# Another idle pattern and another order of the first products in a two-layer encoder trunk

## What is computed

```
def hybrid_layer(x, ...):
    u = rms_norm(x, g_mix_pre)
    proj = u @ w_in            # split into qa, ka, va, cq, ckv, ga, gb
    ...                        # two attentions, gated sum
    x = x + rms_norm(mixed @ w_out, g_mix_post)
    h = rms_norm(x, g_mlp_pre)
    h = jnp.square(jax.nn.relu(h @ w_mlp_in)) @ w_mlp_out
    return x + rms_norm(h, g_mlp_post)
```

## Time and profile before

| | us |
|---|---|
| median of 3 runs | 745.71 |
| lowest and highest run | 745.63, 745.94 |
| the profiled execution | 745.94 |
| its span, first to last instruction | 744.1 |

### The profile page before, as it was taken

The page is one execution under the profiler, slowest core; times in us unless marked ns, Lnnn a source line. Parts: engine busy times, 40 slices in busy tenths (PEclk is TensorE's granted clock), DMA queues, the critical chain, the costliest instruction groups (busy, mean ns, idle before and its releaser), DMA issues.

```text
span 744.1 us, 10940 instructions
## 1 busy us (share of the span) xinstructions
PE 733.6 (99%) x3986; PEld 622.5 (84%) x3986; DVE 503.7 (68%) x710; ACT 415.1 (56%) x783; POOL 157.6 (21%) x256
## 2 busy tenths in 40 slices
PE   8999999999999999999999999999999999999996
PEld 7988888888788888888888888888887888888885
DVE  5787777666775656656686776876668665665664
ACT  6867765343654544444576786644447454455452
POOL 1991432000130111110137513310003110011110
PEclk9999999999999999999999999999999999999999
DMA  7767534455456555456348755346364646655611
GB/s 263 203 211 246 198 114 145 168 198 170 147 193 203 193 177 201 150 204 212 106 115 245 244 162 206 114 135 206 113 226 145 214 153 223 214 181 186 204 62 57
DMA packets 79500, 132.18 MB, mean 178 GB/s; under 512 B 15290, under 2 KB 21476, under 8 KB 79204
## 3 DMA queue, kind: packets, MB, share of 16 engines
q1 hardware_dynamic: 79188, 131.64, 54.0%
q10 hardware_dynamic: 272, 0.00, 0.0%
HBM read 130.59 MB, written 1.05 MB: 177 GB/s over the span
## 4 chain that ended last, share of the span: by engine, by line
PE 94%; DVE 4%; ACT 1%; issue 0%; POOL 0%; DMA 0%; POOLq 0%; ACTq 0%; DVEq 0%
PE acc L1420 17%; PE acc L1422 17%; PE acc L1421 17%; PE sc L1767 7%; PE tp L1767 6%; PE tp L1395 4%; PE sc L1770 3%; PE acc L1454 3%; PE tp L1770 3%; PE sc L1420 3%; PE sc L1422 2%; PE sc L1421 2%; DVE w_lo L1046 2%; PE sc L1552 1%; PE sc L1540 1%; DVE x L1223 1%
## 5 line engine op out<-in xcount | busy, mean ns | idle before, releaser
L1046 DVE TENSOR_TENSOR w_lo<-raw,w_hi 128x1024 fp32r<-128x1024 f32 (+4 forms) x256 | 305.4, 1213 | 152.2 <-ACT w_hi L707 151.3
L707 ACT CAST w_hi<-raw 128x1024 fp32r<-128x1024 f32 (+4 forms) x256 | 250.7, 999 | 173.9 <-PE acc L1422 95.4
L1420 PE MATMUL acc<-w_hi,s_hi 128*128 128x512 f32 x288 | 112.2, 390 | 0.0
L1421 PE MATMUL acc<-w_lo,s_hi 128*128 128x512 f32 x288 | 112.1, 389 | 0.0
L1422 PE MATMUL acc<-w_hi,s_lo 128*128 128x512 f32 x288 | 112.0, 389 | 0.0
L1420 PE MATMUL acc<-w_hi,s_both 128*128 128x512 f32 (+2 forms) x288 | 108.3, 376 | 0.0
L1422 PE MATMUL acc<-w_hi,s_both 128*128 128x512 f32 (+2 forms) x288 | 105.9, 368 | 0.0
L1421 PE MATMUL acc<-w_lo,s_both 128*128 128x512 f32 (+2 forms) x288 | 105.8, 367 | 0.0
L567 POOL TENSOR_TENSOR tok<-relu_h 128x512 f32<-128x512 f32 x32 | 37.0, 1160 | 262.8 <-ACT relu_h L808 257.8
L1767 PE MATMUL sc<-s_both,w_hi 128*128 128x512 f32 x224 | 70.4, 395 | 0.0
L1422 PEld LDWEIGHTS acc<-w_hi,s_lo 128*128 128x128 f32 x288 | 54.1, 188 | 11.3
(11 more groups left out here) (210 smaller groups left out, 1149.8 us busy)
## 6 DMA issues: line engine op xcount, KB each, us to landing
raw<-in_w_mlp_in SPq DMA_DIRECT2D x32, 1024.0 KB, 5.4
raw<-in_w_mlp_out SPq DMA_DIRECT2D x32, 1024.0 KB, 5.0
raw<-in_w_in SPq DMA_DIRECT2D x24, 1024.0 KB, 5.3
raw<-in_w_oa SPq DMA_DIRECT2D x8, 1024.0 KB, 5.0
raw<-in_w_out SPq DMA_DIRECT2D x8, 1024.0 KB, 5.0
raw<-in_w_ob SPq DMA_DIRECT2D x4, 1024.0 KB, 4.9
raw<-in_w_in SPq DMA_DIRECT2D x3, 768.0 KB, 4.6
raw<-in_w_in SPq DMA_DIRECT2D x4, 576.0 KB, 6.2
```

Of the source, the lines that this page charges most:

```text
L707: s.copy(high, src).then_inc(hi_ready, 1)
L1046: v.tensor_tensor(low, src, high, ALU.subtract).then_inc(lo_ready, 1)
L1420: mm(banks[t][:, 0:N], h[:, kk, tk], wh[:, k, :], start=(start and k == 0), stop=False)
L1421: mm(banks[t][:, 0:N], h[:, kk, tk], wl[:, k, :], start=False, stop=False)
```

## The change

Three things change, all in layer 0's head.

The first weight piece is cast by VectorE instead of ScalarE, after the angles; ScalarE starts at piece 1 and first waits for VectorE's cast, so that `hi_ready` counts in order.

In `first_product`, piece 1's high x high products and piece 0's low-weight products now stand ahead of the turn of x's second half; only piece 1's low-weight products stay behind it. This order of the products holds for every call; the turn is there in layer 0's first call alone.

The six plain idle products behind the turn of x's first half become fifteen in the split format fp32r: three with 128 moving columns, six with 64 and six with 256. Their operand is a copy of the identity in that format, twice side by side, made by GpSimd.

```
+        ident_r = sb("ident_r", [P, 2, P], F32R)
...
+            g.tensor_copy(ident_r[:, :, :], ident[:, :].unsqueeze(1).to_broadcast([P, 2, P])).then_inc(ident_r_ready, 1)
...
-                    if pos.l == 0 and pos.j is None and p == 0:
-                        act.wait_ge(first_loaded, 16)
-                    elif p % 2 == 0 or p == 1:
+                    if pos.l == 0 and pos.j is None and p == 1:
+
+                        act.wait_ge(hi_ready, 1)
+                    if p % 2 == 0 or p == 1:
...
                     turned_hi(pos, ("x", 0, 0))
+                    state[0] = 1
                     hi(pos, 1)
...
                     take_angles()
+                    dve.wait_ge(first_loaded, 16)
+                    dve.wait_ge(piece_used, 1)
+                    v.tensor_copy(split_view(w_hi, 0), raw_view(0)).then_inc(hi_ready, 1)
                     lo(pos, 1)
...
+            def idle_split_products():
+
+                pe.wait_ge(ident_r_ready, 1)
+                for _ in range(3):
+                    mm(acc[3][:, 0:P], ident_r[:, 0, :], ident_r[:, 0, :], start=True, stop=True)
+                for _ in range(6):
+                    mm(acc[3][:, 0:CHUNK], ident_r[:, 0, :], ident_r[:, 0, 0:CHUNK], start=True, stop=True)
+                for _ in range(6):
+                    mm(acc[3][:, 0:SEQ], ident_r[:, 0, :], ident_r[:, :, :], start=True, stop=True)
...
                     turn_x(pos, kind, 0, (0,))
-                    idle_product(6)
-                part(0, s1_hi, w_hi, [0], first=True)
+                    idle_split_products()
+                part(0, s1_hi, w_hi, range(2), first=True)
+                part(0, s1_hi, w_lo, [0])
                 if not turned0:
                     turn_x(pos, kind, 0, (1,))
-                part(0, s1_hi, w_hi, [1])
-                part(0, s1_hi, w_lo, range(2))
+                part(0, s1_hi, w_lo, [1])
```

More of the change, by code:

```diff
@@ L295, in build @@
         ident_ready = sem("ident_ready")
+        ident_r_ready = sem("ident_r_ready")
         consts_ready = sem("consts_ready")
```

## The result

| | us |
|---|---|
| before, median of 8 runs | 745.64 (745.45 to 745.94) |
| after, median of 8 runs | 748.2 (746.26 to 748.5) |
| ratio | 1.0029, 95% interval 1.0020 to 1.0039 |
| profiled execution of after, its span | 747.63, 745.8 |

The change costs 2.6 us by the medians, 0.34%; the ratio of 1.0029 lies nearer to that of the means. The forecast was +1.0. One more number in the table matters: before, the runs lie within 0.5 us; after, seven lie at 747.6 to 748.5 and one at 746.26. The profiled execution is 1.7 us longer in its span than that of before (744.1).

A forecast was written before the change was run, and what follows sets the result against it. TensorE bounds the kernel and passes the head's delay on whole. Idle products 0.64 plus products ahead of the turn 1.16 minus 0.78 gave +1.02 us: 746.96 on the profiled execution, 746.7 on the median; range 745.8 to 748.4.

The forecast's parts named there:

- main case: Layer 0's head: idle loads at 0.213 us, real products at 0.175, turn 1.02 us later; +0.8 to +1.4, chance 0.5.
- What bounds the kernel, and that the head passes its delay on: Whole span: TensorE, busy for 99%, bounds it; any delay it has at 20 us reaches the end whole.
- The critical event, the turn of x's second half: Head: ScalarE idles 0.86 us before 9.56 waiting for this turn, then copies out and casts pieces 2 and 3.
- Fifteen idle loads at 0.213: Idle products on TensorE: 15 x 0.213 = 3.20 us, ending at 8.79 instead of 8.15, 0.64 us later.
- The order: `first_product`: a load and six products ahead of the turn take 1.16 us where two took 0.78.
- The clock stays as before: TensorE's head: clock low up to some 8.8 us, high after, so the six products run at 0.175 us each.
- The missed rise: Rival: clock stays low past the turn, which starts 2.0 and ends 2.5 us late; +2.5, 748.2; chance 0.25.
- The cheap rival, narrow products at 0.107: Idle products: loads don't slow with the clock, or columns alone count; +0.44 (746.15) or +0.35; chance 0.2.
- The cast: VectorE casts piece 0 in 0.6 us (lower bound 0.56), ending at 6.5; ScalarE's added wait is already met.
- The cover: Head: piece 0's cast ends at 6.5, 6.9 at the longest, while TensorE's idle products run to 8.79.
- GpSimd's copy: Identity's split copy takes 0.8 us, ending about 3.5; TensorE asks for it at 5.6: hidden, no cost.
- No gain has a path in the head: Head: the order allows the turn at most 0.1 us earlier; no gain above 0.2%, chance of one 0.04.

The follow-up runs named there:

- cast_only: Kernel before with only VectorE casting piece 0 and ScalarE starting at piece 1; idle products and order kept: 745.59 us, ratio 1.0001.
- before_wide12: Kernel before with its twelve plain idle instructions replaced by twelve split idle products of 256 columns: 745.39 us, ratio 0.9997.
- after_narrow15: Changed kernel with all fifteen split idle products 64 columns wide: 748.12 us, ratio 1.0031.
- idle_only: Kernel before with only the fifteen split idle products in place of the twelve plain idle instructions; casts and order kept: 746.69 us, ratio 1.0007.
- after_plain15: Changed kernel with seven plain idle products (fourteen weight loads) and one split one of 256 columns: 746.04 us, ratio 1.0008.

## Why the prediction was right in its range and wrong in its main case

**What bounds the kernel, and that the head passes its delay on**: right. The delay at piece 3, 1.77 us, is the growth of the span, 1.7, and from the restart of TensorE with piece 3 to the end of the span all twelve traces of this case take 731.6 to 731.9 us.

**The critical event, the turn of x's second half**: right. From ScalarE's copy-out of it to the end of the span ten of the twelve traces take 734.3 to 734.6 us. The other two, 734.8 and 734.7, are those in which the cast of piece 2 waited for its load (`cast_only` and `before_wide12`).

**Fifteen idle loads at 0.213**: right to the hundredth, 3.20 us. The stretch ended at 8.54 and not 8.79 since x's first half landed earlier in this execution and the idle stretch began 0.25 us sooner.

**The order**: the step was sound. Alone it measured +0.78.

**The clock stays as before**: this is the step that failed, "six products at 0.175", with "what the clock grants for that no row shows" set aside as a rival. The six took 0.32 us each. The main case took the rise at 8.8 as a fixed time of the head, read from one trace of one execution. The runs show in its place that the rise comes at another time in each execution: the traces of plain and wide patterns have it between about 6 and 8.9, and there it moves the kernel before by no more than some 0.7 us of spread (745.33 to 746.1 over all its runs), as I read it because its products wait for ScalarE's cast until 8.0 in any case; with narrow products in the pattern the three profiled executions had it between 10.4 and 11.0 (the change), between 11.3 and 11.7 (`after_narrow15`), and at about 11.85 (`idle_only`).

The missed rise had been written down as a rival with its price, the turn starting 2.0 and ending 2.5 us late, 748.2, chance 0.25. That is the median measured, and its sign, weight loads of 0.33 us behind 9, stands in the trace. For the profiled execution (747.63, copy-out 1.77 us late) the price is smaller, since the idle stretch began 0.25 us sooner and the clock rose during the turn; no execution near 748.2 was traced, so that the sum comes out to the tenth is in part luck.

So the range held by its rival, not by its main case. It reached only 0.2 beyond the rival's price, and the highest run, 748.5, is above it. A median within 747.2 had been given 0.68 and one above it 0.28; the less likely of the two came.

I had weighed the rival by two observations, that the first stretch had not raised the clock though it was full and that TensorE has no gap in either pattern. The second did not tell the patterns apart: both are busy without a gap in the trace, and only one had the early rise. What differed was the columns, 53 or 107 ns of them in 213 ns; the prediction had these numbers in front of it and gave a late rise behind them a chance of 0.25.

**The cheap rival, narrow products at 0.107**: dead. The Trainium skill (TensorE: Matmul & The Clock Gate, "LDWEIGHTS (loading the stationary operand)") gives a load as columns over 1.2 GHz, with no word of the clock. Here that holds at the high level, 0.11 for 128 columns, but at the low one split loads follow each other in 0.213, and the measurement decides.

**The cast**: cost nothing, as said (745.59 alone). Its duration, 0.56 us, is the lower bound of the prediction. Wrong in detail: the load landed later in this execution, the cast began at 6.41, not 5.95, and ScalarE did wait 0.42 us for it. The cover held, with TensorE in the idle products until 8.54.

**GpSimd's copy**: 0.40 us where I took 0.8; hidden either way.

**No gain has a path in the head**: right for this order, which never gave a run below 745.63. It overlooked the load of pieces 2 and 3, which bounds the old order at 10.14 with an early clock.

## What to carry to other kernels

Work that is there to raise the clock has to be judged by the pace of what follows it, not by how busy the engine looks: here fifteen products with 64 columns behind a full weight load kept TensorE busy throughout, and the clock mostly rose later than behind wide ones. A rise read from one profile is one of several; if a change moves work across it, price the late case fully, and look at the spread of the runs, which shows two groups where a median shows one number. And what stands ahead of an event that another engine waits for delays it by about its full length, even when it fills time in which this engine waits later. Something else can hide part of that: with an early clock the new order has the copy-out 0.80 us later (9.61 in `after_plain15`, 8.81 in `cast_only`), but the cast behind it only 0.48 (10.62 and 10.14), since in the old order it waits for its load.

## What the runs showed of the hardware

- Split products with a 128-column weight load each start 0.213 us apart at the low level, with 64, 128 or 256 columns behind it: fifteen in 3.20 us, mixed or all of 64. Fewer columns gain nothing there.
- With plain or 256-column idle products the slow pace ended between about 6 and 8.9 us in the traces, over different executions of like kernels; with fifteen of 64 columns, or the mix of the change, behind 10.3 in the three traced, and in some runs, by their times, early as well.
- The profile's granted clock reads full speed from the start in all of them; the pace of weight loads shows the low level.
- VectorE casts 768 float32 elements within SBUF, with the change of format, in 0.56 us, where its subtraction of that size takes 0.95. The Trainium skill (VectorE: DVE Perf Modes, "The perf-mode tier table") has an fp32 copy within SBUF at twice the rate of `tensor_tensor`. The trace agrees for the rate of an element: less the 0.195 us of a 64-element instruction, 704 further elements took 0.365 us, 0.52 ns each against 1.03; the whole instruction is 1.7 times as fast.
